# Sample attention of a two-layer decoder step: two batches at a time in column tiles, keys and values streamed in chunks of 512 through a ring of six slots

## The reference, cut to what matters

```python
s_c = einsum('btkgd,bckd->bkgtc', qg, kc)            # scores against 128 compressed blocks
p_c = masked_softmax(s_c, ...)                       # o_c = p_c @ vc
imp = p_c.sum(axis=2) ...                            # importance of the 65 blocks of 64 keys
_, idx = lax.top_k(score, 16)                        # the 16 best blocks, for each key head
s_s = einsum(qg, selected keys); o_s = masked_softmax(s_s) @ selected values
s_w = einsum(qg, window keys and new keys); o_w = masked_softmax(s_w) @ window values
out = gates[0] * o_c + gates[1] * o_s + gates[2] * o_w
```

## Time and profile before

| | us |
|---|---|
| median of 3 timed runs | 2537.17 (2532.31 to 2543.24) |
| profiled execution: span, first to last instruction (the page gives no time beyond it) | 2539.5 |
| cnorm, first instruction to last | 1774.1 to 1791.9 |
| satt, first instruction to last | 1793.3 to 2108.5 |
| busy over the whole span: PE, DVE, ACT | 2018.7, 1014.4, 544.2 |

### The profile page before, as it was taken

How to read it: one execution, slowest core, us unless ns; L and a number is a source line. 1 busy time by engine, 2 the same in 40 slices (tenths; PEclk the granted TensorE clock), 3 DMA queues, 4 the chain that set the end, 5 groups by cost and what they waited for, 6 DMA issues and landing times. The chain is left out here.

```text
span 2539.5 us, 37139 instructions
## 1 busy us (share of the span) xinstructions
PE 2018.7 (79%) x11102; PEld 1449.2 (57%) x11102; DVE 1014.4 (40%) x2457; ACT 544.2 (21%) x1289; POOL 250.7 (10%) x376
## 2 busy tenths in 40 slices
PE   4999878879789577885997678787589898758785
PEld 4888766758567444443885455555144456734443
DVE  2775344453530311112133667676366550221112
ACT  2114632221320211111003333333111110101110
POOL 0000031322210121110000000000000000031110
PEclk8999878878889688996899788888589999879997
DMA  3666440000001669992463201000579872639996
GB/s 127 214 214 199 131 150 36 0 35 0 35 23 62 241 273 425 424 399 104 155 213 127 103 25 44 32 25 25 184 222 287 266 218 75 249 141 425 425 421 228
DMA packets 168254, 443.14 MB, mean 174 GB/s; under 512 B 25905, under 2 KB 97074, under 8 KB 151026
## 3 DMA queue, kind: packets, MB, share of 16 engines
q1 hardware_dynamic: 113954, 384.38, 40.8%
q10 hardware_dynamic: 43216, 39.99, 5.0%
q0 software_dynamic: 11008, 17.89, 1.9%
HBM read 426.45 MB, written 44.03 MB: 185 GB/s over the span
## 5 line engine op out<-in xcount | busy, mean ns | idle before, releaser
L1599 PE MATMUL moe_experts_bank_gu<-moe_weights_gu,moe_experts_xT 128*64 128x256 f32 x2048 | 261.0, 419 | 62.9 <-DMA moe_weights_gu<-in_w_gate_up 44.9
L1599 PEld LDWEIGHTS moe_experts_bank_gu<-moe_weights_gu,moe_experts_xT 128*64 128x64 f32 x2048 | 173.1, 152 | 162.4 <-issue 112.6
L393 PE MATMUL proj_acc<-h_gdn,proj_w 128*128 128x272 f32 x1024 | 237.7, 394 | 14.6 <-DMA proj_w<-in_gdn_w 14.6
L393 PEld LDWEIGHTS proj_acc<-h_gdn,proj_w 128*128 128x128 f32 x1024 | 195.5, 191 | 55.6 <-DMA proj_w<-in_gdn_w 15.0
L1837 PE MATMUL nproj_acc<-nsa_h,nproj_w 128*128 128x272 f32 x640 | 148.2, 395 | 0.0
L1680 DVE SCALAR_TENSOR_TENSOR moe_experts_h<-moe_experts_bank_gu,moe_table,moe_experts_gate 128x128 f32<-128x128 f32 x64 | 22.4, 351 | 299.3 <-ACT moe_experts_gate L1644 299.3
L1620 PE MATMUL moe_experts_bank_y<-moe_weights_down,moe_experts_hT 128*64 128x512 f32 x512 | 116.9, 598 | 25.7 <-ACT moe_experts_hT L1649 25.7
L1837 PEld LDWEIGHTS nproj_acc<-nsa_h,nproj_w 128*128 128x128 f32 x640 | 122.4, 191 | 25.5
L2489 PE MATMUL satt_out_acc<-satt_values,satt_pT 128*64 128x256 f32 x512 | 119.8, 391 | 0.0
L2077 PE MATMUL patt_scores<-nsa_proj,patt_q 128*128 128x128 f32 (+3 forms) x256 | 107.2, 554 | 0.0
L266 DVE TENSOR_REDUCE first_sums<-proj_raw 128x2048 f32 (+1 forms) x32 | 73.2, 2286 | 80.6 <-DMA proj_raw<-in_cmp_pool 80.6
(11 more groups left out here) (425 smaller groups left out, 3466.3 us busy)
## 6 DMA issues: line engine op xcount, KB each, us to landing
moe_weights_gu<-in_w_gate_up SPq DMA_DIRECT2D x64, 2048.0 KB, 20.7
moe_weights_down<-in_w_down SPq DMA_DIRECT2D x64, 1024.0 KB, 22.3
proj_raw<-in_cmp_pool SPq DMA_DIRECT2D x128, 256.0 KB, 3.3
satt_keys<-in_slc_pool SPq DMA_DIRECT2D x256, 128.0 KB, 3.1
satt_values<-in_slc_pool ACTq DMA_DIRECT2D x256, 128.0 KB, 3.4
nproj_raw<-in_cmp_pool SPq DMA_DIRECT2D x80, 256.0 KB, 3.4
proj_w<-in_gdn_w SPq DMA_DIRECT2D x32, 512.0 KB, 3.4
patt_raw<-in_cmp_pool SPq DMA_DIRECT2D x48, 256.0 KB, 2.8
```

Source lines behind the costliest of these rows:

```text
L393: mm = pe.matmul(acc[s][:, a, 0:HALF], w[s][:, k, :], g.hT[:, k, a * HALF:(a + 1) * HALF], start=(k == 0), stop=(k == KT - 1))
L1599: mm = pe.matmul(gu_bank[m][H, 0:FF], ln.xT[:, k, H], w.gu[:, k, m * FF:(m + 1) * FF], start=(k == 0), stop=(k == KT - 1))
```

## The change

Satt now takes two batches at once, in 4 steps, so that rows of two batches fill the 128 partitions; constants, `row_gates` and the buffers grow from 64 rows to 128 (and `row_gates` is spread by 8 transfers, not 4). Keys and values are not held per batch: a class `PageRing` holds six slots of 4 pages for each of the two batches, keys and values together, loaded in transfers of a whole page of 256 KB with rows of 2 KB (the window: 1 MB with rows of 8 KB). SP loads the first batch's pages, ACT the second's. The first six loads are issued in cnorm, ahead of satt. A load for a slot is issued when the slot's products are done.

Each step has 10 chunks: the window, the new keys (with the compressed branch), and 8 of 4 pages. For each chunk PE computes 4 score products of 32 weight columns into the four quarters of the partitions, DVE adds the mask in PSUM and takes the chunk's own maximum, ACT takes the exponential and sums, PE turns the 128 rows, DVE copies, PE multiplies in 16 products of 32 weight columns by 128 value columns (only the two key heads that a quarter needs), and DVE copies the chunk's output to `o_all`. At the end of a step the 11 partial outputs, each with its own maximum, are joined on DVE by 12 operations. POOL has no work left, and the loops over batches are written out.

```diff
-            compress_norm_stage(nc, g)
-            sample_attention_stage(nc, g)
+            with Stage(nc, "kv") as st:
+                rows = PageRing(nc, g, st)
+                compress_norm_stage(nc, g, rows)
+                sample_attention_stage(nc, g, rows)
...
+            @block.sync
+            def _(sp):
+                for r in range(RING):
+                    rows.load(sp, r, 0)
...
                                    ).then_inc(squared, 1)
+                for r in range(RING):
+                    rows.load(act, r, 1)
                 for n in range(4):
                     act.wait_ge(summed, n + 1)
                     act.activation(root[:, n, :], total[:, n, :], ACT.Ln, scale=1.0 / HD, bias=g.eps[:, 0:1]
...
+class PageRing:
...
+    def load(self, eng, r, b):
+        i, c = divmod(r, LOADS)
+        slot = r % RING
+        if c == 0:
+            eng.dma_start(self.rows[:, slot, b, :, :], self.g.d["win"][2 * i + b]).then_inc(self.loaded[b][slot], 16)
+            return
+        at = (2 * i + b) * N_PAGES + (c - 1) * PAGES_C
+        _, pages = self.nc.values_load_multi_w_load_instructions(
+            self.g.page_table[0:1, at:at + PAGES_C],
+            engines=[mybir.EngineType.Activation if b else mybir.EngineType.SP], min_val=0,
+            max_val=N_POOL - 1, skip_runtime_bounds_check_because="the page table holds pages of the pool")
+        for m, page in enumerate(pages):
+            eng.dma_start(self.rows[:, slot, b, m, :],
+                          self.g.d["slc_pool"][bass.ds(page, 1)].rearrange("g p n -> (g p) n")
+                          ).then_inc(self.loaded[b][slot], 16)
...
+                def scores(n):
+                    i, c = which(n)
+                    if c != NEW_CHUNK:
+                        for b in range(2):
+                            pe.wait_ge(rows.loaded[b][load_of(n) % RING], rows.counts[load_of(n)])
+                    if n >= 2:
+                        pe.wait_ge(softened, n - 1)
+                    for b in range(2):
+                        for pair in range(2):
+                            q = g.qb[:, pair, 2 * i + b, :]
+                            R = rows_of(b, pair)
+                            if c == NEW_CHUNK:
+                                mm = pe.matmul(ps[n % 2][R, 0:2 * NEW], q, g.k_new[:, :, pair, :], start=True, stop=True)
+                            else:
+                                mm = pe.matmul(ps[n % 2][R, :], q, rows.keys(n, b, pair), start=True, stop=True)
+                    mm.then_inc(scored, 1)
...
+                        for m in range(PAGES_C):
+                            for b, pair in tiles:
+                                R = rows_of(b, pair)
+                                mm = pe.matmul(bank[R, 0:P], weights[:, m, R], rows.values(n, b, m, pair),
+                                               start=(m == 0), stop=(m == PAGES_C - 1))
...
+                for n in range(ALL_CHUNKS):
+                    i, c = which(n)
+                    if n + 2 < ALL_CHUNKS:
+                        scores(n + 2)
+                    if n + 1 < ALL_CHUNKS:
+                        turn(n + 1)
+                    multiply(n)
...
+                def refill(n):
+                    if n < 0 or which(n)[1] == NEW_CHUNK:
+                        return
+                    r = load_of(n) + RING
+                    if r < PAIR_STEPS * LOADS:
+                        act.wait_ge(summed, n + 1)
+                        rows.load(act, r, 1)
...
+                select(0)
+                soften(0)
+                soften(1)
+                for n in range(ALL_CHUNKS):
+                    i, c = which(n)
+                    if n + 2 < ALL_CHUNKS:
+                        soften(n + 2)
+                    refill(n - 1)
...
+                turn_copied(0)
+                for n in range(ALL_CHUNKS):
+                    i, c = which(n)
+                    if n + 2 < ALL_CHUNKS:
+                        mask(n + 2)
+                    if n + 1 < ALL_CHUNKS:
+                        turn_copied(n + 1)
+                    sum_copied(n)
...
+                    if c == CHUNKS_I - 1:
+                        join(i)
```

More of the change, by code:

```diff
@@ L148, in constants @@
     forced = (blk == 0) | (blk == n_sel - 2)
-    c["forced"] = rows(np.tile(forced * SEL_BIG, (len(row), 1)))
+    c["forced"] = np.tile(forced * SEL_BIG, (len(row), 1))
     return {k: np.ascontiguousarray(v, dtype=np.float32) for k, v in c.items()}
@@ L2312, in sample_attention_stage @@
+def sample_attention_stage(nc, g, rows):
     n_sel = PAST // SEL + 1
@@ L2325, in sample_attention_stage @@
-        score = [st.sb(f"score{n}", [ROWS, n_sel]) for n in range(3)]
-        best = [st.sb(f"best{n}", [ROWS, 8]) for n in range(2)]
-        unselected = st.sb("unselected", [ROWS, n_sel])
-        neg_max = st.sb("neg_max", [ROWS, 3])
-        sums = st.sb("sums", [ROWS, 3])
-        out = st.sb("out", [ROWS, KVH * HD])
-        ps = [st.ps(f"scores{n}") for n in range(2)]
-        ps_cmp, ps_new = st.ps("cmp"), st.ps("new")
-        ps_turn = [st.ps(f"turn{n}") for n in range(2)]
-        ps_out, ps_end = st.ps("out_acc"), st.ps("end")
@@ L2335, in sample_attention_stage @@
-        k_in = [st.sem(f"k_in{c}") for c in range(CHUNKS_KV)]
-        v_in = [st.sem(f"v_in{n}") for n in range(SMP_GROUPS)]
-        win_k_in, win_v_in, cleared = st.sem("win_k_in"), st.sem("win_v_in"), st.sem("cleared")
-        chunks = range(CHUNKS_KV)
-        pe_select = st.steps("pe_select", ["cmp scores", "importance"])
-        pe_score = st.steps("pe_score", [f"scores {c}" for c in chunks] + ["new scores", "win scores"])
-        pe_sum = st.steps("pe_sum", SMP_OUT)
-        pe_end = st.steps("pe_end", ["end"])
@@ new lines, in sample_attention_stage @@
+        acc = st.sb("acc", [P, P])
+        score = [st.sb(f"score{n}", [P, n_sel]) for n in range(3)]
+        best = [st.sb(f"best{n}", [P, 8]) for n in range(2)]
+        unselected = [st.sb(f"unselected{s}", [P, n_sel]) for s in range(2)]
+        cmp_max, cmp_sum = st.sb("cmp_max", [P, 1]), st.sb("cmp_sum", [P, 1])
+        ps = [st.ps(f"scores{s}") for s in range(2)]
+        ps_turn = [st.ps(f"turn{s}") for s in range(2)]
+        ps_out = [st.ps(f"out{s}") for s in range(2)]
+        ps_cmp, ps_end = st.ps("cmp"), st.ps("end")
@@ new lines, in sample_attention_stage, with which, rows_of, masks_before @@
+        dve_join = st.line("dve_join", ["least", "weighed", "whole", "floor", "inverse", "gate", "factor", "factor win",
+                                        "cmp out"] + [f"out {n}" for n in range(PARTS)])
+        ident = g.const("ident")
+        def which(n):
+            return divmod(n, CHUNKS_I)
+        def rows_of(b, pair):
+            at = ROWS * b + NEW * pair
+            return slice(at, at + NEW)
+        def masks_before(n):
+            i, c = which(n)
+            return i * (CHUNKS_I + 1) + c + (1 if c > NEW_CHUNK else 0)
@@ new lines, in end @@
+                def end(i):
+                    pe.wait_ge(dve_join.sem, dve_join.past(f"out {PARTS - 1}", i))
+                    if i:
+                        pe.wait_ge(placed, i)
+                    pe.transpose(ps_end[:, 0:P], acc[:, :], ident).then_inc(ended, 1)
+                select_scores(0)
+                scores(0)
+                scores(1)
+                select_importance(0)
+                turn(0)
+                for n in range(ALL_CHUNKS):
+                    i, c = which(n)
+                    if n + 2 < ALL_CHUNKS:
[3 more added lines that the diff above has]
+                    multiply(n)
+                    if c == 2 and i + 1 < PAIR_STEPS:
+                        select_scores(i + 1)
+                    if c == 5 and i + 1 < PAIR_STEPS:
+                        select_importance(i + 1)
+                    if c == 0 and i:
+                        end(i - 1)
```

596 lines of the change are left out of this document (278 added, 318 removed).

## The result

The changed kernel takes 2437.26 us (median of 4 runs, 2434.41 to 2439.43), the kernel before 2535.91 in the same comparison: a ratio of 0.960 (95% interval 0.958 to 0.963), 4% faster. The forecast was 2451, its range 2420 to 2510. The profiled execution has a span of 2437.2 us, 102.3 less than before. Cnorm's first instruction comes at 1776.9 (before: 1774.1), the end of satt at 2004.2 (before: 2108.5).

A forecast was written before the change was run, and what follows sets the result against it. PE was taken to bound satt after its start, transfers close behind. Satt's end at 2019 saves 89.5 us, less 3.1: 86.4; the span of 2539.5 becomes 2453, the median 2.3 lower: 2451 us, range 2420 to 2510.

The forecast's parts named there:

- Transfers: Page and window loads of cnorm and satt: 75.5 MB unchanged, 210 us at 360 GB/s, bounds 180 to 236.
- Start: Cnorm into satt: ACT's 21 issues take 13 us, satt starts at 1806.5, transfers pause some 7 us.
- small terms: Four more `row_gates` transfers, +2.6 us; one more stage exit, some 0.5; POOL's dropped copies and smaller constants, nothing.
- Tail: Satt after the last landing: chunk 6.5 us, joins 4.6, last turn and placing 1.5; 16 us allowed, with late pages.
- PE: Satt's chunks: 2.9 us each at full clock, 5.2 at half; half clock throughout puts satt's end at 2029.
- I take the middle of the two, 2019: Satt's end, taken between 2008 if transfers alone decide and 2029 with PE at half clock throughout.
- DVE and ACT: Satt, per chunk: DVE 2.75 us, ACT 2.9 to 4.0, both covered by lying under the transfers' 5.8.
- Two quarters: Rival, chance 0.13: PE in satt runs only two tiles at once, 4.75 us per chunk at full clock; 2490 us.
- serial tiles: Rival, chance 0.07: satt's small products go one after another, 8.45 us per chunk at full clock; 2582 us.
- PSUM: Rival, chance 0.06: DVE empties PSUM too slowly in satt, hand-overs 0.5 us, 4.35 us per chunk; 2495 us.
- No gain in rate: Rival, chance 0.06: loads stay at satt's 248 GB/s, taking 304 us; 2533 us, no change.
- The fast end: Rival, chance 0.13: transfers at 390 GB/s or more, PE at full clock, satt's end near 1990; 2422 us.

## Why the prediction was right, and where its sizes were off

**What bounds.** Right. The transfers took PE's place as the bound, shown by the run without refills (49.6 us less) and by PE's doubled work (11 more, not 103).

**Transfers.** Forecast 210 us at 360 GB/s. Measured 33.7 + 167.7 = 201.4 us, 375 GB/s over all and 388 where the engines are busy throughout, as from 1900 to 1950 (share 1.05); the rows of 2 KB run nearer to the experts' 424 than I took. The 358 GB/s of the Trainium skill (DMA: Bandwidth & Descriptors, Where 436 GB/s comes from) is exceeded by this stage also. That issue was the limit of the half pages was my step for the earlier trace rows, and it is wrong: with rows of 1 KB and twice the issues the new order moves 343 GB/s at a share of 1.06, and ACT there issues seven half pages in 3.31 us (from 1895.52), 0.47 each. So the 0.78 us of the earlier trace rows was no price of an issue, but held waits. That PE held the loads back in the kernel before fits this and the earlier trace rows; no run tried it. The row size costs a tenth.

**Start.** The mechanism was right, the size too small. The logarithm came at 1799.7, not 1792, as ACT's 21 issues took 20.1 us (1779.50 to 1799.62) instead of 13; the 0.62 us per issue that I took were kept by the first few only. Satt began at 1813.1 (forecast 1806.5), the first slot came free at 1823.2 (1816), and the pause is 11.6 us, not 7. Of each of these delays 2.8 us are a later start of cnorm, which the sum holds under the small terms. The six loads landed at 1811.6, near the forecast (1810). I did not see that issues by a busy queue also hold the end of their stage; the run with ACT's loads later showed it.

**Tail.** 13.3 us against 16.

**PE.** Its price was right, 2.8 and 5.0 us per chunk against 2.9 and 5.2, and four quarters work at once; but two errors met there. Scores, turning and products take 2.81 us at the full clock, not 2.45, and the 0.15 us for each change of tile shape show in no row: turning begins at 1929.38, when the scores end at 1929.45. The step that failed is "I take the middle of the two, 2019". The transfers alone gave 2008, and satt ended at 2004.2. At half clock PE's chunk (5.0 us) still lies under the 5.4 us that 2.1 MB take at 388 GB/s, and with PE's work doubled the granted clock rose to 0.96 and the stretch by 3% only. Those 11 us are most of the 14 by which the forecast was high. In the profiled span it was high by 15.8: 11 from the middle and 8.6 from the rate, 2.7 from the tail, less 4.6 for the longer pause and 2.0 that the kernel takes longer behind satt (433.0 us after 431.0). The last step, a median 2.3 us below the span, did not hold either, as the median is the span here. That the forecast is high by 0.6% only is thus partly luck: its errors have both signs.

**DVE and ACT.** Right that they lie under the transfers: a chunk takes DVE 0.70 + 0.69 + 0.68 + 0.29 = 2.4 us, and the whole chain without refills 140.

**Small terms.** `row_gates`: eight transfers in 5.14 us where four took 2.60, +2.5, as forecast. The further stage exit costs nothing that shows: from satt's end to the next stage's first transfer it is 2.6 us in both.

**The rivals.** Two quarters and serial tiles: shown wrong by eight score instructions in 1.07 us. PSUM: DVE's masks wait 40.4 us for scores, its two copies 0.6 and 6.4 us for products, and the chain alone needs 140 us: PE does not stand still for DVE's emptying. No gain in rate: wrong, 377 GB/s. The fast end (2422) came nearest: its 390 GB/s were met only where the engines are busy throughout (388; 375 over all), its undisturbed clock was not needed, and the longer pause kept it off. Two of the rivals' sums are off: a step of the PSUM rival is 10 x 4.35 + 13 = 56.5 us by its own terms, not 60, and no gain in rate comes to 2531, not 2533, when it is reckoned like the others.

## What to carry to other kernels

Once the transfers bound a stage, its time is bytes over the measured rate, plus the time in which nothing can be loaded; look for the pauses at its start and end before touching the engines' work. A prefetch issued by a computing engine into a busy queue takes that engine's time and can delay the end of its stage (here by 17 us for the first logarithm and, with ACT's loads later, by 8 us for cnorm's end); issue it from an engine that has nothing to do, and no more of it than lands while the stage works. In a ring, count the slots that are held until a refill can be issued, the place of the refill in its engine's program included.

## What the runs showed of the hardware that was not expected

An issue of a whole page takes 0.5 us at first and 1.0 us behind others in cnorm (18 in 18.14 us), where SP issues too; with ACT's loads later 20 take 14.53 us, 0.73 each. The engines are busy 1.01 in both, so their share alone does not set the pace. An issue to 64 partitions takes 0.64 us, one of the same 128 KB to all 128 takes 0.50. Transfers to 64 partitions of one half run at 268 GB/s with the engines busy 1.06, those to even or odd ones at 308 (share 0.92), those to all 128 at 377 to 388. The Trainium skill (SBUF — State Buffer, Door 1: The DMA port swizzle) gives the half-array transfer 8 of 16 ports, and about half the rate. Here two queues, which may each be in another half, moved 268 of 377 to 388 GB/s, more than half. And PE did nearly twice the instructions in a stretch that grew by 3%, with a granted clock of 0.96 in place of 0.78 and less idle time.
